# Four buffers of transposed probabilities, half projection steps behind the transposes, and two tiles outside the mixers' running sums

## What is computed

```python
for li in range(2):
    mod = silu(c) @ w_ada + b_ada
    h = rms(x, g_pre) * (1 + mod_scale) + mod_shift
    x = x + 0.5 * (1 + mod_gate) * rms(swiglu_1(h), g_post)
    h = rms(x, g_pre) * (1 + mod_scale) + mod_shift
    # layer 0: A (8 heads of 64, chunk band, relative bias) and
    #          B (4 differential heads, ALiBi), one projection in, one out
    # layer 1: C (16 heads of 64, causal, cumulative log-forget bias)
    x = x + (1 + mod_gate) * rms(mixer(h) @ w_out, g_post)
    h = rms(x, g_pre) * (1 + mod_scale) + mod_shift
    x = x + 0.5 * (1 + mod_gate) * rms(swiglu_2(h), g_post)
```

## Time and profile before

| what | value |
|---|---|
| three runs | 2452.78, 2456.75, 2456.69 us, median 2456.69 |
| profiled execution | 2456.77 us, its span 2455.0 us |
| PE busy | 2332.6 us, 95% of the span |
| DVE, ACT, POOL busy | 1448.3, 908.4, 310.4 us |
| mean granted clock of PE | 0.987 of full speed |

### The profile page before, as it was taken

How to read it: one execution, slowest core, us unless ns; L and a number is a source line. 1 busy time by engine, 2 the same in 40 slices (tenths; PEclk the granted TensorE clock), 3 DMA queues, 4 the chain that set the end, 5 groups by cost and what they waited for, 6 DMA issues and landing times.

```text
span 2455.0 us, 45512 instructions
## 1 busy us (share of the span) xinstructions
PE 2332.6 (95%) x18888; PEld 2220.9 (90%) x18888; DVE 1448.3 (59%) x2610; ACT 908.4 (37%) x1964; POOL 310.4 (13%) x373
## 2 busy tenths in 40 slices
PE   7999999999997899999999999997999888999998
PEld 4999999877876899999999999996777788999998
DVE  4577767755556756667566666656555575543223
ACT  3322222455555422222442222334555563222232
POOL 0000002411113300001220000232111161000001
PEclk9999999999998999999999999998999999999999
DMA  7456546322223045445514454442233321432331
GB/s 247 122 163 174 170 125 177 91 70 79 77 69 86 27 121 154 138 127 164 147 45 138 137 153 129 148 124 72 80 89 97 89 81 50 137 104 86 96 87 53
DMA packets 392700, 277.66 MB, mean 113 GB/s; under 512 B 11104, under 2 KB 349824, under 8 KB 392496
## 3 DMA queue, kind: packets, MB, share of 16 engines
q1 hardware_dynamic: 385792, 254.77, 35.6%
q0 software_dynamic: 6704, 19.99, 2.8%
HBM read 263.48 MB, written 12.81 MB: 113 GB/s over the span
## 4 chain that ended last, share of the span: by engine, by line
PE 80%; DVE 10%; ACT 3%; issue 3%; DMA 2%; POOL 2%; SPq 0%; ACTq 0%; DVEq 0%; POOLq 0%
PE lin L1016 59%; PE lin L1271 9%; PE lin L1036 2%; PE ps_s L1321 2%; PE ps_o L1393 2%; PE ps_t L1342 1%; DVE acc L1976 1%; DVE h_lo L2088 1%; DVE neg_max L2412 1%; POOL sums L876 1%; DVE w_lo L1937 1%; DMA raw<-in_ffn_w_down 1%; DVE x L2061 1%; DVE pre L2079 1%; DVE sums L2023 1%
## 5 line engine op out<-in xcount | busy, mean ns | idle before, releaser
L1016 PE MATMUL lin<-h_hi,w_hi 128*128 128x272 f32 x2640 | 566.2, 289 | 9.2 <-DVE w_lo L1937 6.4
L1016 PE MATMUL lin<-h_hi,w_lo 128*128 128x272 f32 x2640 | 563.4, 288 | 0.0
L1016 PE MATMUL lin<-h_lo,w_hi 128*128 128x272 f32 x2640 | 561.3, 288 | 0.0
L1937 DVE TENSOR_TENSOR w_lo<-raw,w_hi 128x1024 fp32r<-128x1024 f32 (+1 forms) x263 | 321.3, 1226 | 313.8 <-ACT w_hi L1509 312.5
L1016 PEld LDWEIGHTS lin<-h_hi,w_hi 128*128 128x128 f32 x2640 | 421.2, 188 | 12.2 <-issue 7.5
L1016 PEld LDWEIGHTS lin<-h_lo,w_hi 128*128 128x128 f32 x2640 | 421.5, 189 | 0.0
L1016 PEld LDWEIGHTS lin<-h_hi,w_lo 128*128 128x128 f32 x2640 | 418.8, 189 | 0.0
L1509 ACT ACTIVATE w_hi<-raw 128x1024 fp32r<-128x1024 f32 (+1 forms) x263 | 270.4, 1037 | 186.3 <-DMA raw<-in_ffn_w_down 148.1
L1976 DVE SCALAR_TENSOR_TENSOR acc<-raw,silu_c,acc 128x512 f32<-128x512 f32 x448 | 314.3, 761 | 0.0
L1016 PE MATMUL lin<-act_hi,w_hi 128*128 128x272 f32 x1296 | 284.9, 290 | 6.5 <-DVE w_lo L1937 6.4
L1016 PE MATMUL lin<-act_lo,w_hi 128*128 128x272 f32 x1296 | 282.8, 289 | 0.0
(11 more groups left out here) (313 smaller groups left out, 3458.6 us busy)
## 6 DMA issues: line engine op xcount, KB each, us to landing
raw<-in_w_ada SPq DMA_DIRECT2D x128, 512.0 KB, 3.8
raw<-in_ffn_w_gate SPq DMA_DIRECT2D x88, 512.0 KB, 3.8
raw<-in_ffn_w_up SPq DMA_DIRECT2D x88, 512.0 KB, 3.8
raw<-in_ffn_w_down SPq DMA_DIRECT2D x64, 448.0 KB, 4.2
raw<-in_ffn_w_down SPq DMA_DIRECT2D x32, 512.0 KB, 4.9
raw<-in_w_in_ab SPq DMA_DIRECT2D x24, 512.0 KB, 3.8
raw<-in_w_in_c SPq DMA_DIRECT2D x24, 512.0 KB, 3.8
start_w<-in_w_ada SPq DMA_DIRECT2D x16, 512.0 KB, 11.7
```

The costliest lines, as they stand in the source:

```text
L1016: m = nc.tensor.matmul(out[a], w_tile(w, k), mv[:, k0 + k, half(a)], start=first and k == 0 and n == 0, stop=last and k == u["tiles"] - 1 ...
L1937: nc.vector.tensor_tensor(w_all(w_l, u["tiles"]), raw_all(u, w_l), w_all(w_h, u["tiles"]).bitcast(F32), ALU.subtract).then_inc(lo_done, 1)
```

## The change

- `empty_probs` uses four buffers for A and C: the two of `probsT` and two laid into `work`, which the stages do not use. It waits for the pair before the last instead of the last one. B keeps two.
- In every stage with a projection, PE does the second half step behind the transposes and the values instead of ahead of them. The turns stay at steps 5, 9, 12.
- ACT copies the transposed probabilities ahead of the inverse sums (`inv_copy`).
- In stage 0 the second turn goes to bank `ps_o`, and the third waits only for the copy of the first.
- In the mixers' tails tiles 6 and 7 are both left out of `sums`, for squares and for x·y; `group_sums` adds three parts. FFN tails keep one tile.
- ACT's and DVE's orders in the mixers' tails: `take` of tiles 5, 6, 7 of half 1 moves ahead, between the rounding of tiles 2, 4 and 5 of the next input, and the split of the fourth head weight moves to the end.
- In the heads of FFNs behind another sublayer, DVE does the split of the last up weight ahead of tile 3 of the next input and of `act_low(j, 0)`.

```diff
@@ -46,10 +46,12 @@
+APART = {"ffn": (7,), "ab": (6, 7), "c": (6, 7)}
...
+TURN_STEPS = {None: (5, 9, 12), "a": (5, 9, 12), "c": (5, 9, 12), "b": (5, 9, 12)}
@@ -644,13 +646,23 @@
-                if st.new is not None and s in (5, 9, 12):
-                    found.append((s, "turn"))
+                if st.new is not None and s in TURN_STEPS[st.att]:
+                    found.append((TURN_STEPS[st.att].index(s), "turn"))
...
+        def turn_bank(st, i):
+            return ps_o if st.st == 0 and i == 1 else ps_t
+        more_probsT = work[:].rearrange("p a n -> p (a n)")[:, 0:2 * SEQ].rearrange("p (s b n) -> p s b n", s=2, n=P)
+        def probs_slot(i):
+            return probsT[:, i] if i < 2 else more_probsT[:, i - 2]
@@ -696,8 +708,9 @@
+            before = sum(2 * (KT - 1 - len(APART[k])) for k in KIND[:j])
...
-            return 2 * (KT - 2) * j + sum(0 < q < KT - 1 for q, _ in order[:order.index((m, a)) + 1])
+            return before + sum(0 < q < APART[KIND[j]][0] for q, _ in order[:order.index((m, a)) + 1])
@@ -863,10 +876,10 @@
-                if q == KT - 1:
+                if q in APART[KIND[j]]:
...
-                if m == KT - 1:
+                if m in APART[KIND[j]]:
@@ -1082,19 +1095,21 @@
-                n = last_before(j, KT - 1, a)
-                last = xy[:, half(n % 2)] if b == 2 else square_slot(n - 2 * KT * j)[:, b, :]
+                parts = [sums[:, a, b, :]]
+                for t in APART[KIND[j]]:
+                    n = last_before(j, t, a)
+                    parts.append(xy[:, half(n % 2)] if b == 2 else square_slot(n - 2 * KT * j)[:, b, :])
...
-                    nc.tensor.matmul(out, mean_w[:, 0:32], sums[:, a, b, c], start=True, stop=False)
-                    m = nc.tensor.matmul(out, mean_w[:, 0:32], last[:, c], start=False, stop=True)
+                    for i, part in enumerate(parts):
+                        m = nc.tensor.matmul(out, mean_w[:, 0:32], part[:, c], start=i == 0, stop=i == len(parts) - 1)
...
-                pe.wait_ge(sq_added, adds(j, a, KT - 2))
+                pe.wait_ge(sq_added, adds(j, a, APART[KIND[j]][0] - 1))
@@ -1275,22 +1290,24 @@
-                def turn(step):
+                def turn(i):
...
-                    if st.st == 0 and step == 5:
+                    if st.st == 0 and i == 0:
...
-                    if step == 5:
+                    if i == 0:
...
-                    elif step == 9:
+                    elif i == 1:
...
-                    n = tr_plan(st).index((step, "turn"))
-                    wait_tr(base + n)
-                    if step in (5, 9):
+                    n = tr_plan(st).index((i, "turn"))
+                    if turn_bank(st, i) is ps_t:
+                        wait_tr(base + (1 if st.st == 0 and i == 2 else n))
+                    if i < 2:
...
-                            m = nc.tensor.transpose(ps_t[:, t * P:(t + 1) * P], src[:, t * P:(t + 1) * P], ident[:])
+                            m = nc.tensor.transpose(turn_bank(st, i)[:, t * P:(t + 1) * P], src[:, t * P:(t + 1) * P],
+                                                    ident[:])
@@ -1408,23 +1425,22 @@
                         m.then_inc(fl_ps, 1)
-                    for s in (5, 9, 12):
-                        turn(s)
+                    for i in range(3):
+                        turn(i)
                     return
...
                 for s in range(STEPS + 2):
-                    if st.new is not None and s in (5, 9, 12):
-                        turn(s)
-                    for part_half in (0, 1):
-                        if st.new is not None and s < LIN_STEPS:
-                            lin_chunk(s, part_half)
-                        if st.st == 8 and part_half == 0 and s in OUT_PART[st.kind]:
-                            m, k = OUT_PART[st.kind][s]
-                            if k == 0:
-                                pe.wait_ge(kv_evac, evs)
-                            if k == max(OUT_PART[st.kind].values())[1]:
-                                pe.wait_ge(o_lo_done, st.at("ot"))
-                            out_part(st.j, m, k)
+                    if st.new is not None and s in TURN_STEPS[att]:
+                        turn(TURN_STEPS[att].index(s))
+                    if st.new is not None and s < LIN_STEPS:
+                        lin_chunk(s, 0)
+                    if st.st == 8 and s in OUT_PART[st.kind]:
+                        m, k = OUT_PART[st.kind][s]
+                        if k == 0:
+                            pe.wait_ge(kv_evac, evs)
+                        if k == max(OUT_PART[st.kind].values())[1]:
+                            pe.wait_ge(o_lo_done, st.at("ot"))
+                        out_part(st.j, m, k)
                     j = s - lag
@@ -1433,6 +1449,8 @@
                         pair_values(j // 2)
+                    if st.new is not None and s < LIN_STEPS:
+                        lin_chunk(s, 1)
                     if s < 10 and s % 2 == 0:
@@ -1651,15 +1669,16 @@
                 take(j, 4, 1)
-                hidden(j + 1, 0, range(2, 4))
+                hidden(j + 1, 0, range(2, 3))
+                take(j, 5, 1)
+                hidden(j + 1, 0, range(3, 5))
+                take(j, 6, 1)
+                hidden(j + 1, 0, range(5, 6))
+                take(j, 7, 1)
+                hidden(j + 1, 0, range(6, KT))
                 split(nxt[3])
-                take(j, 5, 1)
-                hidden(j + 1, 0, range(4, 6))
-                take(j, 6, 1)
-                hidden(j + 1, 0, range(6, KT))
-                take(j, 7, 1)
+                std_out(j, 1)
                 split(nxt[4])
-                std_out(j, 1)
                 split(nxt[5])
@@ -1807,14 +1826,14 @@
-                def empty_turn(step):
-                    n = plan_t.index((step, "turn"))
+                def empty_turn(i):
+                    n = plan_t.index((i, "turn"))
...
-                    if step in (5, 9):
-                        if step == 5:
+                    if i < 2:
+                        if i == 0:
...
-                        dst = (k_nat if step == 5 else v_nat)[:, st.new, 0:QT, :].rearrange("p t n -> p (t n)")
-                        nc.scalar.activation(dst, ps_t[:, :], ACT.Copy).then_inc(tr_out, 1)
+                        dst = (v_nat if i else k_nat)[:, st.new, 0:QT, :].rearrange("p t n -> p (t n)")
+                        nc.scalar.activation(dst, turn_bank(st, i)[:, :], ACT.Copy).then_inc(tr_out, 1)
@@ -1823,15 +1842,18 @@
-                    if q >= 2:
-                        act.wait_ge(pv_done, st.at("pv") + (q - 1 if att == "b" else q // 2))
+                    if att == "b" and q >= 2:
+                        act.wait_ge(pv_done, st.at("pv") + q - 1)
+                    if att != "b" and q >= 4:
+                        act.wait_ge(pv_done, st.at("pv") + q // 2 - 1)
+                    dst = probs_slot(q % 2 if att == "b" else q % 4)
...
-                        nc.scalar.activation(probsT[:, q % 2, 0:t + 1, :].rearrange("p b n -> p (b n)"),
+                        nc.scalar.activation(dst[:, 0:t + 1, :].rearrange("p b n -> p (b n)"),
...
-                        nc.scalar.activation(probsT[:, q % 2, 0:2, 0:DEC],
+                        nc.scalar.activation(dst[:, 0:2, 0:DEC],
...
-                        nc.scalar.activation(probsT[0:DEC, q % 2, 2, 0:DEC], ps_t[0:DEC, 2 * P:2 * P + DEC], ACT.Copy)\
+                        nc.scalar.activation(dst[0:DEC, 2, 0:DEC], ps_t[0:DEC, 2 * P:2 * P + DEC], ACT.Copy)\
@@ -1872,8 +1894,8 @@
                             evac(s // 4 - 1)
-                        if s in (5, 9, 12):
-                            empty_turn(s)
+                        if s in TURN_STEPS[att]:
+                            empty_turn(TURN_STEPS[att].index(s))
                     if st.st == 8 and s in (3, 6):
@@ -1882,12 +1904,12 @@
                         out_hi(j // 2)
+                    j = s - lag
+                    if 0 <= j < 10 and (att != "b" or j % 2):
+                        empty_probs(j, j // 2 if att == "b" else j, lag)
                     j = s - lag - 1
...
                         inv_copy(j // 2)
-                    j = s - lag
-                    if 0 <= j < 10 and (att != "b" or j % 2):
-                        empty_probs(j, j // 2 if att == "b" else j, lag)
                     j = s - lag - 2
@@ -2188,17 +2210,16 @@
                 low(j + 1, 0, 3)
-                split(nxt[3])
                 renew(j + 1, 0, 5)
...
                 low(j + 1, 0, 5)
-                add_squares(j, 6, 1)
                 scale(j + 1, 0, 7)
...
                 low(j + 1, 0, 7)
+                split(nxt[3])
@@ -2226,11 +2247,11 @@
                     product(j, 0)
+                    split(late[1])
                     renew(j, 1, 3)
...
                     act_low(j, 0)
-                    split(late[1])
                     renew(j, 1, 4)
```

(12 more changed lines are left out.)

## The result

The changed kernel takes 2465.41 us (median of 5 runs, 2465.10 to 2470.84) where the kernel before took 2456.70 in the same session (median of 5, 2452.78 to 2457.51). The ratio is 1.0044, its 95% interval 1.0031 to 1.0056: slower by 8.7 us. The prediction had 2464.1, 7.3 us slower. The profiled execution took 2465.41 with a span of 2463.6.

What follows compares the result with a forecast made beforehand. PE, busy 95% of the span, was taken to bound the kernel. From 2456.8 us, stages +24.6, first stages −1.1, mixers' tails −15.0 and FFN head −1.2 summed to +7.3, so 2464.1 us; range 2446 to 2476.

Steps and rivals of the forecast that it cites:

- Stages, +24.6: Stages with a projection: the moved half step lengthens them, C stages 15.0 us in all, A 7.8, B 1.8.
- (1) and (2): C stage, first and second turn: each wait grows 0.75 us; at the first, 0.22 for a copy comes back.
- (3): C stage, step 2: the first transposes, moved forward, meet a new wait of 0.4 to 0.5 us.
- (4): C stage, step 12: the third turn's wait for the copy of the last probabilities goes, 0.38 us back.
- (5): C stage on PE: more changes between kinds of matmuls cost 0.8 us in all, bounds 0 and 1.5.
- First stages, −1.1: First stages: the second turn, in another bank, stops waiting for the first's copy; 1.1 us back in ab, nothing in c.
- Tails, −7.5 each: Mixers' tails: shorter waits and no low-clock stretch, less dearer means and DVE waits, save 7.5 us each, bounds 3 and 9.
- The FFN head behind an FFN, −1.2: FFN head behind an FFN: the late split moved ahead saves 1.68 us less about 0.5, so 1.2.
- The turn waits: Rival at the first two turns: ACT's copy comes half a step sooner, waits do not grow, 2447.6 us; chance 0.15.
- The clock did not fall behind the turns: Rival in the stages: PE's longer waits at turns bring clock falls, 1.7 us each, 2476 or 2483 us; chance 0.10.
- the third rival: Rival in the mixers' tails: only their first two waits go, 3 us each, total 2473 us; chance 0.07.
- The fourth rival: Rival: tails give 9 us each and changes of kind are nearly free, so both cancel, about 2456 us; chance 0.18.

Runs made afterwards that it cites:

- fifth: The changed kernel with ACT's half split of steps 4 and 8 moved behind the copy of the turn that follows: 2458.38 us, ratio 1.0013.
- sixth experiments: The changed kernel with ACT's copies of the first and second turn moved ahead of the exponentials of steps 4 and 8 in A and C stages: 2432.17 us, ratio 0.9894.
- run 23: A count, not a label: the kernel before, with nothing changed, executed 23 times on one chip, took 2451.30 to 2464.71 us.

## Why the prediction held, step by step

**Stages, +24.6.** Right in sum, for two reasons that differ from stage to stage. By the C stage's items (before to after): (1) and (2) the waits grew by 1.01 and 0.81 (predicted 0.75 each), because the queue of ACT ahead of the copy is what ends them; the fifth and sixth experiments show it, by half a microsecond for the split and all of it for the exponential. In A stages the two waits were 0.35 and 0.73 and became 1.35 and 1.54, the same growth; the prediction's "0.7 to 0.9 us" is the longest wait of each of two lines and not their range. The 0.22 of the first turn was no gain: the half step alone, with two buffers, gives the same 36.98 and has no wait at the first turn either. It is in the 1.01, and items 1 and 2 together are 1.60 where the prediction had 1.28. (3) 0.29, predicted 0.45. (4) −0.38, as predicted. (5) PE's time outside its waits went from 32.52 to 33.27, 0.75 more, predicted 0.8; that the changes of kind are what it consists of was not shown. Sum 0.29 + 1.82 − 0.22 − 0.38 + 0.75 = 2.26, as measured; predicted 2.1. Six stages give 13.5. From third turn to third turn the first C stage is 3.74 longer, of which 1.4 is the decay rows' wait, 2.8 before and 4.2 after, that the earlier turns of the first stage only lengthen: 2.3. In all 15.8, predicted 15.0.
The A stages went from 35.48 to 37.55, 2.07 each (predicted 1.95); with 2.0 for the first of them, apart from the 0.5 below, 8.2 in all. The B stages are the wrong term: 30.15 before, 30.11 after, so 0.0 and not 0.6 each. A B stage of the changed kernel still waits at its first turn, for the copy of probabilities, but 0.9 in place of 1.5. Of that 0.64, a new wait of 0.42 for DVE's probabilities takes most, and PE's time outside its waits, 28.43 before and 28.60 after, the rest: the moved half step is paid out of the old wait, wholly. The last C stage kept its length, 32.56 us before and 32.58 after from the third turn ahead of it to the tail.

**First stages, −1.1.** The first one of ab is 1.4 shorter (28.8 to 27.4 from the last mean to the third turn), and 0.5 of it is lost again in the A stage behind it, which the buffers alone show too (32.82 to 33.32). In c nothing is left, as predicted: what the turns gave, the decay rows took.

**Tails, −7.5 each; measured −5.5.** This is the largest term that was mis-sized, and in it the price of the mean's matmuls. Waits: 1.42 + 1.45 + 3.38 + 1.68 = 7.93 before, 0.23 + 0.74 + 0.51 = 1.48 after, 6.45 less; the prediction had 7.9 less 0.4 and 1.2, 6.3. The clock, 0.98 over 91.4 us and 1.00 over 85.9, is worth 1.4 to 1.8, predicted 1.7. But the means cost 1.18 more each, 2.36, and not 0.45 each, 0.9. 6.45 + 1.4 − 2.36 = 5.5. The 0.45 took the price of a matmul from 24 in 0.90 and held it for 36; the price depends on how many parts in a row go to one output. With the other order the 12 more cost 0.30 a mean, less than predicted. The reserve of 0.4 for a faster DVE was not there.

**The FFN head behind an FFN, −1.2.** From 906.95 to 908.49 and from 1281.47 to 1281.85 the changed kernel's lag behind the one before shrinks from 1.54 to 0.38: −1.2. Of that 1.0 fell in the head itself, behind the mean at 1242, and 0.2 ahead of it.

**The sum.** 15.8 + 8.2 − 0.1 − 0.9 − 11.0 − 1.2 = +10.8; the prediction had +7.3, the profiles show +8.6 and the medians +8.7. The rest lies where little or nothing was changed: 0.9 less ahead of the mixer of layer 0, 0.7 between its last stage and its tail, 1.3 in the FFN from 1281 to the next mean, 0.8 behind the second tail, and 1.5 more for one A stage, 39.06 us in place of 37.55: 10.8 − 3.7 + 1.5 = 8.6. So the mechanism of the A and C stages was right and sized within 0.2 us a stage, but that the total came within 1.3 us of 2464.1 is in part luck: the terms missed by 3.5, the tails by 4.0 alone, and 2.2 of it came back in places that the prediction had left out. In two of these places the granted clock is seen to differ: 0.83 before and 1.00 after from 1570 to 1580, and 0.57 after in the long A stage. Such falls change from one execution to the next: the kernel before, run 23 times on one chip, took 2451.30 to 2464.71. That all of the 3.7 is the clock's was not shown.

**The rivals.** The turn waits did grow: the copy of the first turn starts 3.06 us behind the scores, not under 2.3. The clock did not fall behind the turns: all C stages but the first are within 0.03 us of each other. Falls in the first C stage and in the last B stage are there in both kernels. The one fall that the stages of the changed kernel have besides stands 3 us behind the start of an A stage, behind waits of 0.90 and 0.38, and costs 1.5 of a stage; the chunk with it, the same chunk in the next A stage, the window around it, and the window from 1570 to 1580 after and before:

```profile
632.55 2.99 PE lin L1286 x12
...
701.72 1.70 PE lin L1286 x12
...
632.00:636.00 4.00, 4.00 (x18) 3.38 (x18) 0.28 (x1) 0.40 (x2) 3.83 (x6) 0.57 0.49 138
1570.00:1580.00 10.00, 8.47 (x70) 8.39 (x69) 8.44 (x13) 2.05 (x3) 2.06 (x2) 1.00 0.54 158
...
1570.00:1580.00 10.00, 8.48 (x58) 8.40 (x57) 8.09 (x12) 1.35 (x2) 1.68 (x2) 0.83 0.56 163
```

So the price of a fall, 1.7, was about right, and its place was not. By what the Trainium skill, page "TensorE: Matmul & The Clock Gate", section "A second HAM failure mode: psum-queue depth-cycling", tells of another kernel, whose clock swung with frequent short pauses between groups of matmuls, the pauses at the turns should have made the clock swing; 14 waits of 1.7 us in C stages brought no fall. The tails gave 5.5, between the forecast's 7.5 and the 3 of the third rival. The fourth rival did not come true: it had tails of 9 and PE's extra time nearly free, and they were 5.5 and 0.75 a stage. Two terms were off with opposite signs, but others: the B stages cost 1.8 us less than forecast, the tails gave 4.0 less.

The Trainium skill, page "Perfetto Trace Analysis", section "Identifying Performance Opportunities", says that a gap which keeps coming back can mean that there is no room for the next tile. That is not what these gaps were: four buffers alone changed no stage behind the first of a mixer by more than 0.03 us, but for one A stage with a fall of the clock. The one gap that was a lack of a buffer, 0.22, became worth its length only when ACT's order was mended.

## What to carry to other kernels

Before work is moved behind a wait or ahead of it, ask what ends the wait: if that is a chain over other engines which starts at a fixed point, work taken from in front of the wait is paid twice, as idle time and again behind it. Look for an instruction in an engine's queue that stands behind one which it does not need (here a copy behind an exponential that waits for DVE): moving it was worth 22.5 us where four buffers alone were worth none that could be told, and they gained something, 2.9 us, only behind that. When more small matmuls replace a vector addition, price them in the order in which they will run.

## What the runs showed of the hardware

- Small matmuls (68 columns into 32 rows of PSUM) have no fixed price. Counted as the program issues them (the trace has two records for each): with two parts for each group of rows, 24 take 0.90 us; with three parts in a row for one group, 36 take 2.08; with the four groups inside and the parts outside, the same 36 take 1.20. With two parts the order hardly matters (0.90 and 0.85 us for the 24 of an FFN's mean). Why three in a row cost more than two was not tried.
- The moved half step, some four more changes between kinds of matmuls in a C stage, costs PE 0.75 us outside its waits when PE has the two long waits besides (32.52 to 33.27), and 1.3 when it has not (32.05 against 33.34). That the changes of kind are the cause is an inference: PE's time outside its waits also fell by 0.36 when only ACT's copy moved and PE's own order stayed, so some of it hangs on the waits.
- The granted clock falls to half at the same few places, at some of them not in every execution. In the twelve profiles of this case (both kernels and the ten experiments) it fell in the first C stage and late in the last B stage each time, and 3 to 4 us behind the third turn ahead of 14 of 48 A stages, 1.5 us each. It never fell in the 36 B stages with a projection or in the 72 C stages with one behind the first, whether these had two waits of 1.7 or none; in the last C stage, which has more waits (0.2 to 1.7), it fell in two of twelve. A wait's length alone does not tell whether the clock falls behind it: behind waits of 2.37 and 2.34 at the same place in mixer c's head, it fell before and not after. What does was not settled.
